# Normed activations and all tiles above them lie 32 bytes further up in a two-block transformer kernel

## The reference

```python
for li in range(DEPTH):                       # 2
    x = x + 0.5 * _swiglu(_rmsnorm(x, g[0]), ffn_w_in[li, 0], ffn_w_out[li, 0])
    x = x + mixer(_rmsnorm(x, g[1]))          # recurrence, then latent attention
    x = x + 0.5 * _swiglu(_rmsnorm(x, g[2]), ffn_w_in[li, 1], ffn_w_out[li, 1])
    gate = sigmoid(_rmsnorm(x, g[3]) @ ple_w_gate[li])
    x = x + gate * (p[li] @ ple_w_in[li])
```

## Time and profile before

| | |
|---|---|
| median of 3 runs | 1582.22 us (1576.25 to 1585.52) |
| the profiled execution: time, span | 1582.22 us, 1580.4 us |
| TensorE matmul busy | 1510.2 us, 96% of the span |
| VectorE busy | 1107.7 us, 70% |
| ScalarE busy | 781.5 us, 49% |
| GpSimd busy | 205.5 us, 13% |
| mean granted clock of TensorE | 0.980 of full speed |
| moved by DMA | 264.86 MB, mean 168 GB/s |

### The profile page before, as it was taken

The page is one execution under the profiler, slowest core; times in us unless marked ns, Lnnn a source line. Parts: engine busy times, 40 slices in busy tenths (PEclk is TensorE's granted clock), DMA queues, the critical chain, the costliest instruction groups (busy, mean ns, idle before and its releaser), DMA issues.

```text
span 1580.4 us, 31078 instructions
## 1 busy us (share of the span) xinstructions
PE 1510.2 (96%) x12279; PEld 1453.6 (92%) x12289; DVE 1107.7 (70%) x1648; ACT 781.5 (49%) x1259; POOL 205.5 (13%) x239
## 2 busy tenths in 40 slices
PE   6999998999999999999999999999988998989988
PEld 6999998989999999999989799999978976889767
DVE  5876568986896577876577746975578458394583
ACT  5544355455554356544352735644454448254481
POOL 1111013711331010111010001101023000120000
PEclk9999999999999999999999999999988999999999
DMA  7786744244786646876644244876556503085010
GB/s 225 230 258 218 251 135 134 81 134 148 233 273 227 213 136 189 263 229 213 206 124 143 81 161 154 285 237 221 169 160 171 167 14 107 1 246 173 13 55 27
DMA packets 219309, 264.86 MB, mean 168 GB/s; under 512 B 22253, under 2 KB 197325, under 8 KB 219213
## 3 DMA queue, kind: packets, MB, share of 16 engines
q1 hardware_dynamic: 209136, 234.58, 47.5%
q0 software_dynamic: 8960, 27.37, 5.2%
q10 hardware_dynamic: 1117, 1.57, 0.3%
HBM read 262.44 MB, written 1.05 MB: 167 GB/s over the span
## 4 chain that ended last, share of the span: by engine, by line
PE 77%; DVE 13%; ACT 5%; DMA 3%; issue 2%; another core or an unknown queue 0%; SPq 0%; POOL 0%; DVEq 0%; ACTq 0%
PE bank L1063 22%; PE bank L1064 22%; PE bank L1065 22%; DVE w_lo L1733 4%; DMA w_raw<-in_ffn_w_in 2%; PE bank L1633 1%; PE bank L1470 1%; PE bank L1666 1%; ACT w_hi L690 1%; DVE rs L1762 1%; PE bank L1484 1%; ACT sq L712 1%; PE bank L1482 1%; DVE hg_s L1951 1%; PE bank L1667 1%
## 5 line engine op out<-in xcount | busy, mean ns | idle before, releaser
L690 ACT ACTIVATE w_hi<-w_raw 128x1024 fp32r<-128x1024 f32 x452 | 455.3, 1040 | 457.7 <-PE bank L1065 282.2
L1063 PE MATMUL bank<-xh,w_lo 128*128 128x256 f32 x2312 | 649.9, 281 | 22.9 <-DVE xl L2221 13.3
L1733 DVE TENSOR_TENSOR w_lo<-w_raw,w_hi 128x1024 fp32r<-128x1024 f32 x452 | 547.9, 1248 | 155.4 <-ACT w_hi L690 154.7
L1064 PE MATMUL bank<-xl,w_hi 128*128 128x256 f32 x2312 | 645.2, 279 | 0.0
L1065 PE MATMUL bank<-xh,w_hi 128*128 128x256 f32 x2312 | 644.9, 279 | 0.0
L1063 PEld LDWEIGHTS bank<-xh,w_lo 128*128 128x128 f32 x2312 | 437.5, 189 | 27.6 <-DVE xl L2221 14.3
L1065 PEld LDWEIGHTS bank<-xh,w_hi 128*128 128x128 f32 x2312 | 437.7, 189 | 0.2
L1064 PEld LDWEIGHTS bank<-xl,w_hi 128*128 128x128 f32 x2312 | 436.7, 189 | 1.1 <-issue 0.7
L1063 PE MATMUL bank<-hh,w_lo 128*128 (+1 forms) x704 | 196.4, 279 | 0.0
L1064 PE MATMUL bank<-hl,w_hi 128*128 (+1 forms) x704 | 196.1, 279 | 0.0
L1065 PE MATMUL bank<-hh,w_hi 128*128 (+1 forms) x704 | 196.1, 279 | 0.0
(11 more groups left out here) (368 smaller groups left out, 2190.6 us busy)
## 6 DMA issues: line engine op xcount, KB each, us to landing
w_raw<-in_ffn_w_in SPq DMA_DIRECT2D x176, 512.0 KB, 4.7
w_raw<-in_ffn_w_out SPq DMA_DIRECT2D x88, 512.0 KB, 4.3
w_raw<-in_w_in SPq DMA_DIRECT2D x52, 512.0 KB, 4.7
mod_raw<-in_w_ada POOLq DMA_DIRECT2D x128, 192.0 KB, 4.4
w_raw<-in_a_w_in SPq DMA_DIRECT2D x32, 512.0 KB, 4.3
w_raw<-in_ple_w_gate SPq DMA_DIRECT2D x16, 512.0 KB, 4.4
w_raw<-in_b_w_out SPq DMA_DIRECT2D x16, 512.0 KB, 3.7
w_raw<-in_w_out SPq DMA_DIRECT2D x16, 512.0 KB, 3.5
```

What stands on the lines that cost most here:

```text
L690: A(w_hi[:, c % NSLOT, cols], w_raw[:, c % NRAW, cols], ACT.Copy).then_inc(*did(hi_ready))
L1063: mm(out, lhs[1], rhs[0], start=start, stop=False, skip_group_check=skip)
L1064: mm(out, lhs[0], rhs[1], start=False, stop=False, skip_group_check=skip)
L1733: V.tensor_tensor(w_lo[:, c % NSLOT, cols], w_raw[:, c % NRAW, cols], f32(w_hi[:, c % NSLOT, cols]), ALU.subtract).then_inc(*did(lo_ready))
```

## The change

One line moves the address at which `xh` is placed by 32 bytes, and with it all that comes after: `xl` and every tile from `region` on. The sizes stay multiples of 64, so all these tiles now begin 32 bytes past a step of 64. Tiles before `xh`, and those that are overlaid on `sq` or on the key latent tiles, keep their place.

```diff
     gpre = fixed("gpre", [P, KD])
     gpost = fixed("gpost", [P, KD])
     ptok = fixed("ptok", [P, 2, TB, T])
+    base[0] += 32
     xh = fixed("xh", [P, KD, T], F32R)
     xl = fixed("xl", [P, KD, T], F32R)
     region = base[0]
```

## The result

The changed kernel takes 1614.94 us (median of 4 runs, 1614.46 to 1615.86), the kernel before 1582.77 us (4 runs, 1576.25 to 1585.52): ratio 1.0202, 95% interval 1.0174 to 1.0230. It is 32 us slower, 2 us above the top of the range and far outside the forecast's own 1573 to 1592.

What follows compares the result with a forecast made beforehand. TensorE's matmuls, covering 96% of the span, were taken as the bound. Streamed products, DMAs and other engines each added 0, so the sum stayed at 1582.2 us: predicted 1582, own range 1573 to 1592, range with mild rivals 1560 to 1613.

Steps and rivals of the forecast that it cites:

- Step (1): TensorE's 10,488 products with one operand moved to a half step of 64 bytes: 0 us taken.
- Its bounds, -76 to +44 us: Limits for the moved products: 7.2 ns each regained down to 107.8 ns, or 3.7% (4.2 ns) each lost.
- The two nearest TensorE rows show nothing.: 24-column gate chunk, 117.4 ns with every second slice on a half step; compression, 221 ns at all offsets: support for 0.
- The distance already changes sign between `columns` and `tokens` without a third pace.: Distance between streamed and weight tile differs in sign between the two functions, yet no third pace appears: support for 0.
- The third support: Memory lines are 16 bytes by the Trainium skill, so 32 bytes are two whole lines and nothing moves: support for 0.
- The reading of before: TensorE's long streams: 113.3 and 117.7 ns at full clock, a phase entered after a gap and kept until the next.
- The estimate that the phases alone move the total by some 5.6 us: Over twelve long TensorE stretches, half of each one's possible 3.8% difference, added as squares, gives some 5.6 us.
- R1's mild form: Slower rival: streamed rows cross one extra 64-byte step, all products take the long pace, 29 us more, 1611; chance 0.15.
- R2: Faster rival: half a step ends a collision of streamed and weight rows; 18 us less, 1564, or 76, 1506; chance 0.19.
- The reason I gave against R2: Paces differ without any difference in addresses, so timing alone sets them and a new offset shifts both phases alike.
- Steps (2) and (3): DMAs of moved tiles: 0, at most 3 us. VectorE, ScalarE and GpSimd on moved tiles, far from the bound: 0.
- a new, third pace would prove the forecast wrong whatever the total: Sign laid down for TensorE's long unbroken stretches, where the forecast had only 113.3 and 117.7 ns, both present.

Runs made afterwards that it cites:

- m1: Table kernel without the computation, TensorE alone: 18 cases of streamed and held starts and widths; 120.0 ns with both tiles at 0, 116.7 with streamed 32 further.
- m2: Table kernel without the computation: streamed tile 0 to 512 bytes past the held one in steps of 32, seven draws each; paces 116.7 to 120.0 ns, repeating after 256 bytes.
- m5: Table kernel without the computation: held tile at 128, fine distances, wait of another length in each draw; 113.9 ns at 112, 113.5 or 117.8 at 192.
- e1: Kernel before with the same tiles moved by 64 bytes, so streamed tiles stay on whole steps, d = 0: 1627.66 us, ratio 1.0274.
- e3: Kernel before with the weights moved 32 bytes and everything above them 64, streamed tiles on whole steps, d = 224: 1616.90 us, ratio 1.0204.
- e2: Kernel before with every tile, weights too, 32 bytes higher, all on half steps, d = 192 as before: 1582.88 us, ratio 0.9992.
- e8: Kernel before with the same tiles moved by 96 bytes, on half steps of 64, d = 32: 1601.79 us, ratio 1.0111.
- m3: Table kernel without the computation: held tile at 128, streamed 0 to 240 bytes further in steps of 16, plus 184 to 200; 113.5 to 114.7 ns at 112.

## Why the prediction was wrong

Step (1) failed. It took 0 for the streamed products, and they took 3.3 ns more each, 118.3 instead of 115.0, 35 us in all. Its bounds, -76 to +44 us, held the true +32, but by luck: the upper one came from a copy on VectorE, and the lower one from an unstalled stream of 107.8 ns that no run shows. The fastest product of 256 columns seen took 113.3 ns, and even 128 columns beside a full load took 111.7 (m1). The value 0 rested on two reasons, and both broke.

"The two nearest TensorE rows show nothing." They couldn't. In the earlier trace rows the held row has 24 columns, and m1 shows that such a short load changes the pace by itself, 120.0 to 113.4 ns at one streamed address; its slices also lie 96 bytes apart, so its distances run through several values and 117.4 is a mean over them (the second such chunk of the same trace has 114.4). In the earlier trace rows the 221 ns are shown durations, which aren't a pace; 64 of these products take 3.86 us, 60 ns each, while 30 plain fp32 columns by the rate of the earlier trace rows are only 25 ns. The stream isn't what bounds them, so a stall in it can't show. Rows without the full-size load beside a full-rate stream were neighbours in name only.

"The distance already changes sign between `columns` and `tokens` without a third pace." True, and worthless: with a period of 256 bytes, 192 turned round is 64, and these two share the same two paces (m2, m5). The sample of distances in the trace was in effect one pair. The third support, that 32 bytes are two whole lines of 16 and so nothing moves, fell with the result itself: they cost 3.3 ns a product, and even 4 bytes count (m5). What I had no means to know was the period; what I could have seen is that two values don't describe a function.

The reading of before was right: two paces at one clock and one alignment, a phase that is kept until the next break. m5 shows it with nothing around it. The estimate that the phases alone move the total by some 5.6 us (4.9 from the eleven stretches listed) fits the spread as well. When the change left only one pace that spread fell to 1.4 us; e1 and e3, with one pace each, spread by 2.8 and 2.4 us, and e2, with the two of before, by 19 us in ten runs.

R1's mild form, 1611 us, came near the time by the wrong mechanism. It had all products take the long pace because a row crosses one 64-byte step more; the pace was a new one, and e2 and e8 on half steps refute the step. R2 named the right mechanism, a collision of the streamed row with the weight row, with the wrong sign: half a step of offset made it worse, and the offset that helps is another. The reason I gave against R2, that timing alone sets the paces, is the error of the case: the addresses set which phases exist, and at one set of addresses only the draw among them changes from break to break.

Steps (2) and (3) held: `mod_raw` 37.0 to 37.4 us, other engines within 1.6 us busy. The signs laid down beforehand worked too: "a new, third pace would prove the forecast wrong whatever the total", and it stood in the first stretch read.

## What to carry over

For fp32r matmuls like these, 256 streamed columns and 128 new weight columns each, the distance modulo 256 bytes between the streamed and the held tile is a size to tune: here between 113.3 and 123 ns a product, and 56 us of a kernel (45.6 + 10.7) between d = 0 and d = 112. Put d at 112 (or, with two paces, at 192), not at 0, where tiles with equal starts land, and look at it whenever a tile ahead of either changes its size. Find it with a table kernel that runs TensorE alone, and read paces by counting starts in unbroken stretches, not by the mean duration of a group, which here rose only from 281 to 285 ns.

## What was not expected of the hardware

- Four bytes matter: 119.8, 113.9 and 122.0 ns at d = 108, 112 and 116 (m5); a streamed tile 4 bytes past its weights took 123.2 ns (m1), and none was slower.
- Absolute place isn't quite nothing at 16 bytes: both tiles at 16 gave 118.3 ns, both at 0 or both at 32 gave 120.0 (m1). At d = 32 a held start of 0 gave 116.7 in every draw (m2), one of 128 gave 116.8 or 117.8 in turn (m3). No run followed this up.
- At one set of addresses two paces exist, 113.3 and 117.8, and hold for 48 or for over a thousand products. What in a break decides between them stays open: at d = 192 in m5 the waits of 0.215 and 0.228 us gave the long pace, those of 0.206, 0.219 and 0.235 us the short one.
- How the memory serves the two reads (what is shared, which of the two waits, and why 112 is fast while 96 and 128 are not) is not settled by these runs. That the distance to the held tile sets the pace, and that the size of the load takes part, is shown; why this function of the distance, is not.
